# Residual columns transposed straight onto the output projection's banks

## The reference

```python
u = rms_norm(h, g_mix[l])
...
g_a, g_r = jnp.split(jax.nn.sigmoid(gates + b_gate[l]), 2, axis=-1)
h = h + (g_a * y_a + g_r * y_r) @ w_out[l]
...
xq = (rms_norm(h, g_cross[l]) @ w_xq[l]).reshape(B, S, X_HEADS, X_HEAD_DIM)
```

## Time and profile before

| | |
|---|---|
| median of 3 runs | 1805.42 us (1804.56 to 1806.05) |
| span of the profiled execution | 1807.1 us |
| TensorE (PE) busy | 1759.0 us, 97% |
| VectorE (DVE) busy | 1087.8 us, 60% |
| GpSimd (POOL) busy | 982.2 us, 54% |
| ScalarE (ACT) busy | 698.0 us, 39% |
| mean DMA rate | 145 GB/s |

### The profile page before, as it was taken

One profiled execution on the slowest core, in us unless ns is written; L12 is line 12 of the kernel. 1 busy time (PEld: TensorE's weight loads), 2 busy tenths in 40 slices (PEclk: granted clock), 3 DMA queues, 4 the chain that ended last, 5 costly groups with the idle time before them and its releaser, 6 DMA issues.

```text
span 1807.1 us, 25034 instructions
## 1 busy us (share of the span) xinstructions
PE 1759.0 (97%) x8599; PEld 1467.8 (81%) x8599; DVE 1087.8 (60%) x1535; ACT 698.0 (39%) x1243; POOL 982.2 (54%) x554
## 2 busy tenths in 40 slices
PE   7999999999999899999999999999999999999998
PEld 7888888888888677788878888778888888878887
DVE  5655663002334778884345564887777777889842
ACT  7422223111013667731133232644444444444432
POOL 6743333445654577654433232577777777655540
PEclk9999999999999999999999999999999999999999
DMA  6511111347661789583221134243433334494322
GB/s 266 204 52 36 36 43 49 139 164 256 227 227 46 276 317 325 177 308 113 103 71 59 59 104 141 77 139 107 142 117 123 133 110 139 142 344 143 122 76 93
DMA packets 111245, 262.33 MB, mean 145 GB/s; under 512 B 7744, under 2 KB 50368, under 8 KB 106688
## 3 DMA queue, kind: packets, MB, share of 16 engines
q1 hardware_dynamic: 84720, 182.13, 30.3%
q10 hardware_dynamic: 26448, 79.18, 11.8%
HBM read 186.82 MB, written 73.92 MB: 144 GB/s over the span
## 4 chain that ended last, share of the span: by engine, by line
PE 84%; DVE 6%; ACT 5%; issue 2%; DMA 1%; POOL 1%; ACTq 0%; DVEq 0%; SPq 0%; POOLq 0%
PE ps L714 16%; PE ps L719 16%; PE ps L720 16%; PE ps L1333 7%; PE ps L1338 7%; PE ps L1335 7%; PE ps L1408 2%; PE ps L1409 2%; PE ps L1410 2%; ACT prow L1792 2%; PE ps L1110 1%; PE ps L1090 1%; DMA raw<-in_slabs 1%; DVE aneg L2570 1%; PE ps L1431 1%
## 5 line engine op out<-in xcount | busy, mean ns | idle before, releaser
L609 POOL TENSOR_SCALAR wh<-raw 128x1024 fp32r<-128x1024 f32 x75 | 211.6, 2822 | 467.3 <-PE ps L714 448.9
L714 PE MATMUL ps<-uh,wh 128*128 128x512 f32 x560 | 221.2, 395 | 0.7 <-POOL wl L602 0.7
L720 PE MATMUL ps<-uh,wl 128*128 128x512 f32 x560 | 218.4, 390 | 0.0
L719 PE MATMUL ps<-ul,wh 128*128 128x512 f32 x560 | 218.0, 389 | 0.0
L611 POOL TENSOR_TENSOR wl<-raw,wh 128x1024 fp32r<-128x1024 f32 x75 | 182.0, 2427 | 6.3
L646 POOL TENSOR_TENSOR wl<-raw,wh 128x512 fp32r<-128x512 f32 x88 | 137.5, 1573 | 69.1 <-ACT wh L1457 67.8
L633 POOL TENSOR_TENSOR over_rings<-over_rings 128x512 f32<-128x512 f32 x92 | 118.2, 1285 | 51.5 <-DMA over_rings<-in_slabs 45.9
L1457 ACT ACTIVATE wh<-raw 128x512 fp32r<-128x512 f32 (+1 forms) x164 | 105.4, 656 | 88.9 <-PE ps L1338 58.0
L689 POOL TENSOR_TENSOR wl<-raw,wh 128x512 fp32r<-128x512 f32 x63 | 93.7, 1496 | 78.2 <-ACT wh L1457 78.2
L2212 DVE SCALAR_TENSOR_TENSOR ya<-zA,sm,ya 128x512 f32<-128x512 f32 x88 | 109.6, 1246 | 31.7 <-ACT ya L2036 24.6
L720 PEld LDWEIGHTS ps<-uh,wl 128*128 128x128 f32 x560 | 105.1, 188 | 22.6
(11 more groups left out here) (488 smaller groups left out, 4873.9 us busy)
## 6 DMA issues: line engine op xcount, KB each, us to landing
raw<-in_slabs SPq DMA_DIRECT2D x110, 512.0 KB, 3.6
over_rings<-in_slabs SPq DMA_DIRECT2D x22, 1024.0 KB, 7.1
s_s<-over_rings SPq DMA_DIRECT2D x22, 1024.0 KB, 4.9
ssm<-s_s SPq DMA_DIRECT2D x22, 512.0 KB, 4.5
raw<-s_s SPq DMA_DIRECT2D x22, 512.0 KB, 3.8
s_f<-yb ACTq DMA_DIRECT2D x22, 512.0 KB, 5.3
raw<-s_d SPq DMA_DIRECT2D x36, 256.0 KB, 2.5
dsum<-in_slabs SPq DMA_DIRECT2D x16, 512.0 KB, 6.7
```

The costliest lines, as they stand in the source:

```text
L609: pool.tensor_scalar(wh[:, j, :], raw[:, j % RAWS, :], 1.0, None, ALU.mult).then_inc(S["w_hi"], 1)
L714: l = pe.matmul(o, lh, rh, start=start, stop=False)
L719: pe.matmul(o, lh, rl, start=False, stop=False)
L720: return pe.matmul(o, ll, rh, start=False, stop=stop)
```

## The change

The scratch `s_x`, the tiles `xtile` and `xst`, and `x_rows`, `x_turn` and `x_copy` go. `residual_in(m)`, issued by ScalarE, loads 128 columns of `x` for all 1024 tokens into `hT[:, m, :]`: for blocks 0 and 1 ahead of the mix, for block m + 2 behind mix block m. TensorE waits for all eight loads, then `residual(m)` transposes four tiles of a block's half onto its bank, the first of them starting the accumulation, and the projection's products add to them. VectorE only copies the bank to `hT`, over the rows just read. The projection's loop of four slabs is written out. The counts of `x_ld0` to `x_ld3` follow, and the first `dsum` loads wait for the last retention output (`y_lo`) instead of the stores.

```diff
-        (xtile,) = place(120, [("xtile", [P, CH, D], 0)])
-        (xst,) = place(140, [("xst", [P, 4, 2, H2], 0)])
...
-            ("b21", 0, "x_ld1", 48), ("b21", 1, "x_ld2", 48), ("b21", 2, "x_ld3", 48),
+            ("b21", 0, "x_ld1", 16), ("b21", 1, "x_ld2", 16), ("b21", 2, "x_ld3", 16),
...
                 if n == 9:
-                    sp.wait_ge(S["mm_ld"], 16 * MB + 128)
+                    sp.wait_ge(S["y_lo"], 2 * RH)
...
             def dense(..., ready=None, bank=0, lead=None):
...
                     at_least(pe, d_free[b], u)
+                    if lead:
+                        lead(b)
                     for k in range(nk):
...
+                        l = mm3(ps[0:m, bank + b, :], ..., not lead and k == 0, k == nk - 1,
+                                freed if first and b == k == 0 else 0, onto=lead is not None)
...
-            def x_turn(n):
-                b, k = divmod(n, KB)
-                if k == 0:
-                    for t in range(CH):
-                        pe.wait_ge(S[f"x_ld{t}"], 32 + 16 * b)
-                if n >= 4:
-                    pe.wait_ge(S["mm_hi"], KB + n - 3)
-                for t in range(CH):
-                    l = pe.transpose(ps[:, 2 + n % 4, t * P:(t + 1) * P], xtile[:, t, k * P:(k + 1) * P], ident)
-                l.then_inc(S["mm_t"], 1)
...
+            def residual(m):
+                def rows_in(b):
+                    for j in range(CH):
+                        c = slice((CH * b + j) * P, (CH * b + j + 1) * P)
+                        pe.matmul(ps[:, b, j * P:(j + 1) * P], hT[:, m, c], ident, start=j == 0, stop=False,
+                                  is_transpose=True, skip_group_check=True)
+                return rows_in
+            pe.wait_ge(S["x_ld0"], 16 + 16 * KB)
             dense_late(0, SLAB0["out"], USE0["out"], KB, of(mih, mil),
-                       lambda k, b: pe.wait_ge(S["mix_lo"], 2 * k + b + 1))
-            for j in range(1, 4):
-                dense(j, SLAB0["out"] + j, USE0["out"] + j, KB, of(mih, mil))
-            with pe.Fori(1, KB // 4) as i:
-                for j in range(4):
-                    dense(j, SLAB0["out"] + 4 * i + j, USE0["out"] + 4 * i + j, KB, of(mih, mil))
+                       lambda k, b: pe.wait_ge(S["mix_lo"], 2 * k + b + 1), residual(0))
+            for m in range(1, KB):
+                dense(m % SLOTS, SLAB0["out"] + m, USE0["out"] + m, KB, of(mih, mil), lead=residual(m))
...
-            def x_rows(b):
-            def x_copy(n):
...
-            act.wait_ge(S["mm_ld"], 16 * MB + 128)
+            def residual_in(m):
+                act.dma_start(hT[:, m, :].rearrange("p (t n) -> p t n", t=NT),
+                              x[:, m * P:(m + 1) * P].rearrange("(t p) n -> p t n", p=P)).then_inc(S["x_ld0"], 16)
+            for m in range(2):
+                residual_in(m)
             for m in range(KB):
...
-                act.dma_start(hT[:, m, :], s_x[m]).then_inc(S["x_ld0"], 16)
+                if m + 2 < KB:
+                    residual_in(m + 2)
...
-                    dve.tensor_tensor(hb, ps[:, bank + b, :], res(b), ALU.add).then_inc(d_free[b], 1)
+                    if res is None:
+                        dve.tensor_copy(hb, ps[:, bank + b, :]).then_inc(d_free[b], 1)
+                    else:
+                        dve.tensor_tensor(hb, ps[:, bank + b, :], res(b), ALU.add).then_inc(d_free[b], 1)
...
-            dve.wait_ge(S["x_ld0"], 48 + 16 * KB)
...
-            dve.wait_ge(S["x_ld0"], 48 + 16 * KB + 16)
+            dve.wait_ge(S["x_ld0"], 16 + 16 * KB + 16)
```

More of the change, by code:

```diff
@@ L710, in _, with mm3 @@
         def _(pe):
-            def mm3(o, lh, ll, rh, rl, start, stop, freed=0, extra=None):
-                l = pe.matmul(o, lh, rh, start=start, stop=False)
+            def mm3(o, lh, ll, rh, rl, start, stop, freed=0, extra=None, onto=False):
+                l = pe.matmul(o, lh, rh, start=start, stop=False, skip_group_check=onto)
                 if freed:
@@ L718, in mm3 @@
                     extra()
-                pe.matmul(o, lh, rl, start=False, stop=False)
-                return pe.matmul(o, ll, rh, start=False, stop=stop)
+                pe.matmul(o, lh, rl, start=False, stop=False, skip_group_check=onto)
+                return pe.matmul(o, ll, rh, start=False, stop=stop, skip_group_check=onto)
             def wslot(j, k, n=P, at=0, width=None):
@@ L727, in dense @@
             def dense(j, s, u, nk, act, width=P, at=0, m=P, freed=1, first=True, between=(None, None),
-                      ready=None, bank=0):
+                      ready=None, bank=0, lead=None):
                 if first:
@@ L737, in dense @@
                             ready(k, b)
-                        l = mm3(ps[0:m, bank + b, :], *wslot(j, k, m, at, width), *act(k, b), k == 0, k == nk - 1,
-                                freed if first and b == k == 0 else 0)
+                        l = mm3(ps[0:m, bank + b, :], *wslot(j, k, m, at, width), *act(k, b), not lead and k == 0, k == nk - 1,
+                                freed if first and b == k == 0 else 0, onto=lead is not None)
                     l.then_inc(d_done[b], 1)
@@ L917, in _, with gates_and_heads @@
             for j in range(4):
-                x = 4 * (j - 2)
-                dense(j, SLAB0["ga"] + 4 + j, USE0["ga"] + 4 + j, KB, of(uh, ul),
-                      between=(x_turns(x), x_turns(x + 2)) if j >= 2 else (None, None))
+                dense(j, SLAB0["ga"] + 4 + j, USE0["ga"] + 4 + j, KB, of(uh, ul))
             pe.wait_ge(S["y_lo"], 2 * RH)
-            def gates_and_heads(i, turns=None):
+            def gates_and_heads(i):
                 for j in range(4):
                     s, u = SLAB0["gr"] + 4 * i + j, USE0["gr"] + 4 * i + j
-                    x = KB + 4 * (j - 2)
-                    between = (x_turns(x), x_turns(x + 2)) if turns and j >= 2 else (None, None)
                     if j % 2 == 0:
-                        dense(j, s, u, KB, of(uh, ul), between=between)
+                        dense(j, s, u, KB, of(uh, ul))
                     else:
-                        dense(j, s, u, RH, of(yth, ytl), between=between)
-            gates_and_heads(0, True)
+                        dense(j, s, u, RH, of(yth, ytl))
+            gates_and_heads(0)
             for k in range(KB):
@@ L1639, in gate_a @@
                     act.dma_start(row(s_ga, m), sig[:, p, :]).then_inc(S[f"g_st{p}"], 16)
-            def x_rows(b):
[L1643 to L1646, removed]
-            def x_copy(n):
[L1650 to L1659, removed]
             order(RH, lambda j, b: gate_a(j, b, j % 2), last=True)
-            x_rows(0)
             for m in range(4, KB):
@@ L2694, in h0_block @@
             def h0_block(m):
[L2695 removed]
+                resid(0, m, USE0["out"] + m + 1, hT, None, acc, sq, g0h, g0l,
                       "g_cross")
             clear(0, acc)
[L2698 removed]
             h0_block(0)
```

16 lines of the change are left out of this document (3 added, 13 removed).

## The result

The changed kernel takes 1813.18 us (median of 5 runs, 1811.96 to 1817.55). The kernel before, timed beside it, takes 1805.2 us (median of 5, 1803.38 to 1806.05). The ratio is 1.0047, with a 95% interval of 1.0034 to 1.006 (it is taken from all runs, so it isn't quite the quotient of the medians): slower by 8.0 us in the medians, where 5.5 us were forecast. The time lies in the range, above its middle.

A forecast was written before the change was run, and what follows sets the result against it. TensorE, busy 97% of the span, was taken as the bound. Transposes +0.3, seam wait +3.6 and clock +1.6 gave +5.5 us, 1805.4 to 1810.9 us; the 8-in-10 range was 1804.3 to 1814.5.

The forecast's parts named there:

- Transposes: TensorE: eight groups leave the gates, saving 7.0 us; sixteen enter the output projection, costing 7.3; net +0.3 us.
- Rival (d): Output projection: added transposes fall into TensorE's waits for banks while the gates save 7.0 us; 1798.4 us, chance 0.08.
- VectorE's copy: Output projection: the add of bank and residual becomes a copy; gain between 0 and 1.0 us, taken as 0.
- The hold of ScalarE: Mix: residual 2's issue, the third small-piece load, holds ScalarE some 8 us, until the twelfth 4 KB load lands at 795.5.
- rival (a): Mix: residual 1 and 2 are both held until 795.5; seam wait about 9.8 us, total 1817 to 1819, chance 0.08.
- The delay of VectorE: Mix: the held third copy makes VectorE's low part 3.9 us late, with no idle time to catch up.
- The wait at the seam: From mix to output projection: TensorE idles 3.6 us until VectorE empties the mix's last bank.
- The wait for all eight loads: Ahead of the output projection: last residual load lands by 819.7, hidden below the wait for VectorE ending at 821.3.
- The clock: After the seam wait TensorE's granted clock falls to 0.50, costing 1.6 us, bounds 0 and 3.3.
- (b): Mix: ScalarE is not held, so the change only moves the transposes; +0.3, 1805.7 us, chance 0.30.
- (c): Seam: ScalarE not held, but TensorE waits 0 to 3 us for the last residual load; say 1807 us, chance 0.06.
- the rule of the room on the queue: DMA queue: room for three small-piece loads, the third let in once what lies ahead of the first two has landed.

The follow-up runs named there:

- the experiment: zero_early without the 64 transposes, the residual loaded and waited for but not added: 1796.83 us, ratio 0.9956 to the kernel before.
- zero_early: Changed kernel with TensorE waiting for each residual block separately and each residual load issued behind its own mix block: 1805.34 us, ratio 1.0003.
- kb_pieces: Changed kernel with its eight residual loads cut into 512 pieces of 1 KB each, not adding the true residual: 1808.69 us, ratio 1.0017.
- one_early: Changed kernel with separate waits per residual block and each load issued one mix block ahead, only one before the mix: 1806.94 us, ratio 1.0013.
- big_pieces: Changed kernel with each new load fetching 128 whole rows in 4 KB pieces, not adding the true residual: 1807.2 us, ratio 1.0009.
- zero_early_all: zero_early with the changed kernel's single wait for all eight residual loads ahead of the projection: 1814.87 us, ratio 1.0052.
- sync_queue: Changed kernel with the eight residual loads issued by SyncE between its slab loads instead of by ScalarE, single wait kept: 1805.83 us, ratio 1.0001.
- per_block: Changed kernel with TensorE waiting for each residual block before its own transposes instead of for all eight at once: 1812.98 us, ratio 1.0043.
- fill_wait: Changed kernel with 19 filler products into an unused bank where TensorE waits ahead of the projection: 1812.2 us, ratio 1.0034.

## Why the prediction came out right

Its sum was +5.5 us; the medians say +8.0, and the terms, measured one by one, +7.3. The chain of causes was the forecast one. But 5.5 lies below the interval of the ratio (+6.1 to +10.8 us), so the sum was short, by 0.7 us at the wait and 1.05 at the clock; and that it was no further off is in part luck, as the delay of VectorE shows below.

**Transposes: as said.** Of 7.0 us forecast for the gates, some 7.1 are there: the last transposes ahead of them start 0.28 us earlier in the changed kernel (330.36 for 330.64), the first behind them 7.40 (417.86 for 425.26). That the table above has 7.0 at 602.71 is chance, since the clock falls a little earlier there in the changed kernel's trace. Of 7.3 added, 7.53 by the experiment. One group near the stage's end, read as in the earlier trace rows:

```profile
906.41 0.39 PE L717 MATMUL ps<-mih,wl 128*128 128x512 f32 x1
906.64 0.60 PE L1169 MATMUL ps<-cn,hT 128*128 128x128 f32 x4
...
907.32 0.39 PE L716 MATMUL ps<-mil,wh 128*128 128x512 f32 x1
```

That is 0.91 less 0.454, 0.46 us, exactly that of the earlier trace rows. Rival (d), that they fall into waits, is out.

**VectorE's copy: as said.** Worth nothing: the 0.3 us wait for it stands in the list after as before.

**The hold of ScalarE: right in kind, wrong in which load.** The sentence that failed is "residual 0 and 1 (784.2; two, taken as quick)". Residual 1 was held already, for 6.57 us, and residual 2, forecast at some 8 us, for 3.60, though it did end with the landing of the twelfth 4 KB load. I had carried over from SyncE that room for three such loads matters, and SyncE's row had one 4 KB load ahead, not twelve. So this is half of rival (a), which I had given 0.08: the second load is held too, but not until the twelfth load has landed, only until the ninth has. That is 3.7 us sooner, most of what separates the measured time from its 1817.

**The delay of VectorE: nearly right by luck, since two errors cancel.** I said 3.9 us for the third copy, with nothing to catch up. Measured against zero_early, the same program with no hold, VectorE's first low part is 6.2 us late (784.94 against 778.71), its third 3.9 (788.80 against 784.89), and its emptying of the last bank 4.6 (814.02 against 809.41). It did catch up, in these two instructions of zero_early, which take 0.69 us elsewhere and which the changed kernel doesn't have there:

```profile
778.71 1.52 DVE L2173 TENSOR_TENSOR mil<-sa,mih 128x512 fp32r<-128x512 f32 x1
...
782.80 2.17 DVE L2607 TENSOR_TENSOR sa<-sa,mr 128x512 f32<-128x512 f32 x1
```

The surplus is 2.3 us, all of what was made up between the first low part and the third. Both begin in the time in which GpSimd splits a slab (778.34 to 784.41), when the changed kernel's VectorE was idle. The window that I read as "busy 11.83 of 12 us" holds the same two, 1.52 us at 786.04 and 2.17 at 790.13. A busy engine isn't an engine without slack when some of its instructions take two or three times their usual time. The Trainium skill, page "SBUF — State Buffer", section "SBUF: two separate sides", says that VectorE with two inputs from this memory and a GpSimd operation share a pair of ports that one of them holds for a whole instruction; both instructions have two such inputs, and the trace agrees in that. It doesn't bear out the whole instruction, as far as GpSimd's records can be trusted: the slowed one at 778.71 ended at 780.23, within a GpSimd instruction that ran to 781.43, and one at 780.87, with two such inputs as well, took 0.69. No run here isolates GpSimd as the cause.

**The wait at the seam:** 4.3 us, forecast 3.6, for the reason given: 4.6 us of delay in place of 3.9, less the 0.3 of slack that the forecast took. **The wait for all eight loads** was said to be hidden beneath, and was, by 0.6 us. That a wait of this kind can cost as much by itself was not said, and "Without the delay it would land at 815.9", in time, is not tested with 512-byte pieces issued in this order: in kb_pieces, where VectorE was nearly in time, TensorE waited 2.1 us for that load.

**The clock:** 2.65 us, forecast 1.6, with 0 and 3.3 as bounds. It fell, as said. Mis-sized is its length: I took the 3.2 us stretch of the earlier trace rows, and it was 6.8 us, like that row's longest; 1.5 of these fell in the wait itself and cost nothing, so 5.3 us of work ran at half the clock. In the traces here 1.54 us of idle time at this seam left the clock at 1.00 (one_early) and 2.1 us did not (kb_pieces). The earlier trace rows calls 1.93 us TensorE's longest wait, which it isn't: at 7.77 us in the kernel before TensorE had waited 7.8 us for VectorE, and the clock was at 1.00 from there to 30 us. So not every long wait was followed by a low clock.

**The total.** +0.3, +4.3 and +2.65 make +7.3 us. The interval of the ratio is +6.1 to +10.8 us. One slip in the working changed nothing: a gain of 1.0 us under (b) gives 1804.7 as the lower end, not 1804.3.

**Rivals.** (b), no hold, is refuted by the rows above, and big_pieces shows what it would have looked like: it is true of 4 KB pieces. With it goes, for this queue and these pieces, the sentence of the Trainium skill ("DMA: Bandwidth & Descriptors", "Anatomy of one DMA") that a lot of descriptors come before the cost shows; it speaks of another path, and ScalarE's trace shows 6.57 us for one load. (c), a wait for the last load, wasn't what TensorE met, but zero_early_all shows it as real, 6.0 us.

**Settled:** the loss is ScalarE held at DMA issues cut into 512-byte pieces, which delays VectorE, which stops TensorE, whose clock then falls; beneath lies the wait for all eight loads. Without both, no gain or loss can be measured (zero_early, sync_queue). No version that adds the residual beat the kernel before, since moving 64 transposes moves their full cost.

**Open:** the rule of the room on the queue. In four traces (after, per_block, one_early, fill_wait) the second 512-byte load is let in between the landings of the ninth and the tenth of twelve 4 KB loads and the third within 0.5 us of the twelfth's; no simple count of pieces fits these and kb_pieces together.

## What to carry to other kernels

A DMA issue is an instruction of the engine that issues it, and when the load is cut small and many loads are outstanding on its queue it can last for microseconds; look at what stands behind it in that engine's program before putting it there, and give such loads to a queue with nothing urgent behind them, or issue them after the urgent work. When a stall is found at a seam, ask which wait comes next beneath it: here finer waits alone (per_block) and later issues alone (zero_early_all) gained nothing, and both together (zero_early) gave the whole loss back. And read a gain in TensorE's work only from its own stream: transposes moved from one stage without gaps to another cost the same there.

## What the runs showed of the hardware

- An issue of one 512 KB load in 1024 pieces of 512 bytes took 0.46 us as the first behind twelve 4 KB loads, 6.57 us as the second, 3.60 and 1.69 as the third and fourth. In 4 KB pieces the same issues took 0.35 to 0.5 us; in 1 KB pieces the second and third took 1.73 and 4.28. SyncE was held in the same manner (5.08 us).
- Two VectorE instructions of 0.69 us took 1.52 and 2.17 us when they began while GpSimd worked on a slab, and the delayed VectorE of the changed kernel escaped both. A later one took 2.88 us in the changed kernel and zero_early alike (792.77 and 792.72).
- In the wait of 4.3 us at the seam TensorE's granted clock went to 0.50 near 813.35 us, 1.5 us before work went on, and was back at 1.00 near 820.16. With filler products for 4.6 us of the gap, and 1.56 us idle behind them, it stayed at 1.00.
